# Modulation rows of a one-core backbone layer: the sum over k on GpSimd, one matmul by ones on TensorE

## The reference, cut to what matters

```python
mod_lat = (jax.nn.silu(c) @ w_mod[l] + b_mod[l])[:, None, :]
sh1, sc1, gt1, sh2, sc2, gt2 = jnp.split(mod_lat, 6, axis=-1)
...
yx, _, _ = _token_mixer(hx, st_fwd, st_bwd, True, True, **mp)
x = x + gt1 * _rmsnorm(yx, ng[1])
...
hx = _modulate(_rmsnorm(x, ng[2]), sh2, sc2)
x = x + gt2 * _rmsnorm(_peer(hx, ...), ng[3])
```

## Time and profile before

| | |
|---|---|
| median of 3 runs | 2881.05 us (2877.75 to 2894.06) |
| span of the profiled execution, the only time that is known of it | 3458.3 us |
| granted TensorE clock in it | 0.555 |
| TensorE busy | 3369.1 us (97%) |
| VectorE busy | 1668.8 us (48%) |
| GpSimd busy | 1188.9 us (34%) |
| ScalarE busy | 614.5 us (18%) |
| stage 4 in it | about 530 to 1480 us |

### The profile page before, as it was taken

How to read it: one execution, slowest core, us unless ns; L and a number is a source line. 1 busy time by engine, 2 the same in 40 slices (tenths; PEclk the granted TensorE clock), 3 DMA queues, 4 the chain that set the end, 5 groups by cost and what they waited for, 6 DMA issues and landing times.

```text
span 3458.3 us, 29585 instructions
## 1 busy us (share of the span) xinstructions
PE 3369.1 (97%) x8354; PEld 1703.9 (49%) x8354; DVE 1668.8 (48%) x3954; ACT 614.5 (18%) x1385; POOL 1188.9 (34%) x1143
## 2 busy tenths in 40 slices
PE   8999999999999999989899999999999999999998
PEld 3333327999999999935533333222222222222222
DVE  1167503455545455452533443466555555555661
ACT  2043200011011110121111111212222221222121
POOL 3000000000000000000444434767676877677772
PEclk6555555555555555555555555555555555555555
DMA  4122212122111111041777766889997999889994
GB/s 153 33 83 98 86 36 73 37 54 69 37 50 37 49 38 37 13 152 36 253 264 260 276 223 227 316 306 361 352 338 284 346 360 350 307 334 364 342 334 158
DMA packets 266271, 650.77 MB, mean 188 GB/s; under 512 B 21280, under 2 KB 120192, under 8 KB 265856
## 3 DMA queue, kind: packets, MB, share of 16 engines
q0 software_dynamic: 150336, 552.67, 44.0%
q1 hardware_dynamic: 115776, 96.28, 9.3%
HBM read 631.04 MB, written 17.83 MB: 188 GB/s over the span
## 4 chain that ended last, share of the span: by engine, by line
PE 96%; DMA 2%; ACT 1%; issue 1%; DVE 1%; SPq 0%; ACTq 0%; DVEq 0%; PEldq 0%
PE bank L1269 46%; PE bank L1749 10%; PE bank L780 5%; PE bank L765 5%; PE bank L778 4%; PE bank L1281 4%; PE bank L963 3%; PE bank L718 3%; PE bank L1751 2%; PE bank L1722 1%; PE bank L739 1%; PE bank L688 1%; PE bank L1014 1%; PE bank L786 1%; PE bank L750 1%; PE bank L745 1%
## 5 line engine op out<-in xcount | busy, mean ns | idle before, releaser
L1269 PE MATMUL bank<-arena 128*128 128x512 f32 x2048 | 1577.5, 967 | 25.6 <-DVE arena L1231 19.5
L1269 PEld LDWEIGHTS bank<-arena 128*128 128x128 f32 x2048 | 464.0, 227 | 1130.4 <-issue 1114.1
L1250 DVE CUSTOM_DVE_ANT_0 arena<-arena 128x1024 f32<-128x1024 f32 x512 | 608.5, 1225 | 537.2 <-DMA arena<-in_peer_u_dram,arena 537.2
L1062 POOL DMA_INDIRECT arena<-in_peer_v_dram,arena x512 | 577.0, 1127 | 364.7 <-PE bank L1269 222.6
L1062 POOL DMA_INDIRECT arena<-in_peer_u_dram,arena x512 | 565.3, 1104 | 302.6 <-issue 135.9
L1095 ACT ACTIVATE arena<-arena 128x128 f32<-128x128 f32 x512 | 201.8, 401 | 1172.1 <-PE bank L1269 1164.2
L1749 PE MATMUL bank<-arena 128*128 128x512 f32 x432 | 349.6, 968 | 6.2 <-PEq L381 3.5
L825 POOL MEMSET arena<- 128x4096 f32 x1 | 3.5, 3517 | 954.8 <-DVE arena L613 954.8
L780 PE MATMUL bank<-arena 128*128 128x128 f32 x960 | 207.3, 392 | 0.0
L765 PE MATMUL bank<-arena 128*128 128x128 f32 x960 | 197.1, 384 | 0.1
L780 PEld LDWEIGHTS bank<-arena 128*128 128x128 f32 x960 | 194.6, 302 | 0.0
(11 more groups left out here) (279 smaller groups left out, 2668.6 us busy)
## 6 DMA issues: line engine op xcount, KB each, us to landing
arena<-in_w_mod_dram SPq DMA_DIRECT2D x24, 1024.0 KB, 6.2
arena<-in_peer_wq_dram SPq DMA_DIRECT2D x32, 512.0 KB, 6.4
arena<-in_w_in_dram SPq DMA_DIRECT2D x27, 512.0 KB, 4.1
arena<-kr_scratch SPq DMA_DIRECT2D x96, 128.0 KB, 3.5
arena<-in_peer_u_dram,arena POOLq DMA_INDIRECT x512, 6.1
arena<-in_peer_v_dram,arena POOLq DMA_INDIRECT x512, 6.1
bk_scratch<-arena POOLq DMA_DIRECT2D x8, 768.0 KB, 3.6
kr_scratch<-arena POOLq DMA_DIRECT2D x8, 768.0 KB, 5.0
```

Of the source, the lines that this page charges most:

```text
L1062: pool.indirect_dma_start(ring[:, j % RING, :], None, table, bass.IndirectOffsetOnAxis(ap=idx[:, hi % 4, j:j + 1].bitcast(U32), axis=0)).t ...
L1250: nc.vector.tensor_tensor_reduce(u_ring[:, j % RING, :], u_ring[:, j % RING, :], h2cur, 1.0, 0.0, ALU.mult, ALU.add, acts[:, h % 2, j:j + ...
L1269: m = nc.tensor.matmul(PO[h][:, :], diag[:, j % 4], v_ring[:, j % RING, 512 * h:512 * h + 512], start=hp == 0 and j == 0, stop=hp == HEADS ...
```

## The change

GpSimd now multiplies the loaded block by silu(c), in place, and adds up its eight values of k in three halving steps, the last of them into `row_sum`, which has two buffers. TensorE does one matmul, with a 128x128 tile of ones, which sums over the partitions and spreads the result. `row_steps` counts GpSimd's steps, four for a row: TensorE waits for the fourth instead of the weights' landing, and SP's next load of `wmr` waits for GpSimd's fourth step instead of TensorE's matmul. GpSimd waits for the matmul of two rows earlier before it writes `row_sum`. The `silb` tile and its copy are gone; `ones` takes one memset more. No instruction changes its place against others on an engine.

```diff
     wmr = cut(KT, 256)
-    silb = cut(KT, P)
+    row_sum = cut(2, 256)
+    ones = cut(P)
+    cut = Cut(MOD + 2048 + D, ARENA - 2048)
     rows = cut(4, D)
...
-                    sp.wait_ge(modulation_rows, 4 * p + j)
+                    sp.wait_ge(row_steps, 16 * p + 4 * j)
                     apart(sp)
                 sp.dma_start(wmr, wmod_v[:, :, bass.ds(p * D + (2 * D + 256 * j), 256)]).then_inc(wmod_row_weights, 16)
...
-        nc.gpsimd.tensor_copy(silb, silu_col[:, :, 0:1].broadcast_to([P, KT, P])).then_inc(silu_spread, 1)
+        nc.gpsimd.memset(ones, 1.0).then_inc(n_zeroed, 1)
+
+        def weighted_row(p, j, first):
+            n = 4 * p + j
+
+            pool.wait_ge(wmod_row_weights, 16 * n + 16)
+            nc.gpsimd.tensor_tensor(wmr, wmr, silu_col[:, :, 0:1].broadcast_to([P, KT, 256]), ALU.mult).then_inc(row_steps, 1)
+            pool.wait_ge(row_steps, 4 * n + 1)
+            nc.gpsimd.tensor_tensor(wmr[:, 0:4], wmr[:, 0:4], wmr[:, 4:8], ALU.add).then_inc(row_steps, 1)
+            pool.wait_ge(row_steps, 4 * n + 2)
+            nc.gpsimd.tensor_tensor(wmr[:, 0:2], wmr[:, 0:2], wmr[:, 2:4], ALU.add).then_inc(row_steps, 1)
+            pool.wait_ge(row_steps, 4 * n + 3)
+            if not (first and j < 2):
+                pool.wait_ge(modulation_rows, n - 1)
+            nc.gpsimd.tensor_tensor(row_sum[:, j % 2], wmr[:, 0], wmr[:, 1], ALU.add).then_inc(row_steps, 1)
+
+        def do(p, b, chain, first):
+            for j in MOD_BLOCKS[b]:
+                weighted_row(p, j, first)
+        steps4(pool, do, lambda: None)
...
             if first and j == 0:
-                pe.wait_ge(silu_spread, 1)
+                pe.wait_ge(n_zeroed, 7)
...
-            pe.wait_ge(wmod_row_weights, 64 * p + 16 * j + 16)
-            for k in range(KT):
-                m = nc.tensor.matmul(C1[j % 2][:, P:P + 256], silb[:, k, :], wmr[:, k, :], start=k == 0, stop=k == KT - 1)
-            m.then_inc(modulation_rows, 1)
+            pe.wait_ge(row_steps, 16 * p + 4 * j + 4)
+            nc.tensor.matmul(C1[j % 2][:, P:P + 256], ones, row_sum[:, j % 2], start=True, stop=True).then_inc(modulation_rows, 1)
```

More of the change, by code:

```diff
@@ L322, in _layer @@
     wmod_row_weights = sem("wmod_row_weights")
-    silu_spread = sem("silu_spread")
+    row_steps = sem("row_weighting_steps")
     modulation_rows = sem("modulation_rows")
```

## The result

| | before | changed |
|---|---|---|
| median of 5 runs each | 2885.37 us | 2906.59 us |
| ratio, 95% interval | | 1.0076 [1.0048, 1.0104] |
| span of the profiled execution | 3458.3 us | 2905.0 us |
| mean granted clock in it | 0.555 | 0.900 |

The change makes the kernel slower by 21 us, 0.76%, outside the forecast range. The two profiled executions can't be laid side by side: that of the kernel before ran with a mean granted clock of 0.555 and took 3458.3 us. Every later execution of it had 0.907 to 0.965. The clock of its five timed runs wasn't recorded, but they were as short (2877.75 to 2894.06 us) as the later ones on the first chip, which had 0.91 (2866.42 to 2901.19 us). The first experiment therefore profiles the kernel before again.

What follows compares the result with a forecast made beforehand. TensorE, busy 97%, was taken to bound the kernel, with only work to win. Heads 15 plus third-block slots 18 minus collisions 2 gave 31 us less, 2881 - 31 = 2850 us (-1.1%), range 2818 to 2878.

Steps and rivals of the forecast that it cites:

- 15 + 18 - 2: Stage 4: 15 us saved in block heads, 18 in the third blocks' slots, 2 lost to collisions, 31 us less.
- What bounds the kernel, and the clock of the runs: Whole kernel: TensorE busy 97%, no idle time to win; runs need 0.83 of the profiled time, estimated clock 0.67.
- The remark that the expert stage could shorten by at most a sixth: Expert stage: already moves 304 GB/s against 364 in its best slice, so other stages may have run faster than 0.67.
- The slot in the head: Block heads, 12 of 16 rows: VectorE's chain of 12.4 us becomes the limit; 1.4 us saved each, 11 counted, 15 us.
- VectorE is already the limit: Rival, in the heads: from a clock of 0.74 the twelve head slots give nothing; 2865 to 2873 us, 25 in 100.
- The slot in the third block: Third blocks, 4 rows: VectorE has little to do, so the whole 4.5 us a row is saved, 18 us.
- GpSimd's price: GpSimd in stage 4: two reads an element, 7.8 us a row, hidden except at the first row, counted as nothing.
- In the way: VectorE beside GpSimd in stage 4: only the last, short sums meet an L587; 2 us charged, ends nothing and 30.
- the narrow collision: GpSimd holds up only L587, at most 1.9 us a row; rival where every one is held: 2878 us, 5 in 100.
- its own sign of it: In the changed profile: L587 exceeding 0.35 us often would show the forecast wrong by narrow collision.
- the bound of 30: Upper end of the collision charge in stage 4: 16 rows at 1.9 us each.
- The wide collision: Rival: GpSimd's reads hold up every VectorE instruction, PSUM operand or not; 2891 to 2930 us, 10 in 100.

Runs made afterwards that it cites:

- The first experiment: The kernel before, unchanged, profiled again at the clock of the runs: 2890.79 us in one run, stage 4 621.7 us.
- where it stood alone: Against the kernel before: no GpSimd sums, constant rows, one matmul in the third blocks' four slots, eight in the heads: 0.9934, stage 4 612.3 us.
- the example above: Timeline of one block's head in the changed kernel: one matmul at 419.59, 2.02 us idle, clock at 0.5 from 422.2 to 429.0; whole kernel 1.0076.
- beside the eight matmuls: The kernel before with its eight matmuls a row, plus GpSimd's four operations a row into a tile nobody reads: 2918.02 us, stage 4 640.9.
- filled heads and thin slots: The changed kernel with its GpSimd sums, the matmul by ones repeated eight times in each head, once in the third blocks' second slot: 1.0054, stage 4 646.3 us.

## Why the prediction was wrong

The forecast was 31 us less; measured were 21 us more. The sum "15 + 18 - 2" failed in all three of its terms, and a fourth was missing. The heads gave nothing instead of 15 us, because the clock of the runs was wrong; the third blocks' slots gave 9.4 instead of 18; the collisions cost 15.3 us of stage 4 instead of 2; and a lower clock behind the thinned heads, which the sum had at nothing without a word on it, cost 13.3. The first mistake alone would have left a gain; it is the last two that turned the sign.

**What bounds the kernel, and the clock of the runs: the first step that failed.** The prediction took the whole's ratio of 0.83 as one factor for TensorE's work and arrived at a clock of 0.67. The clock of later executions as short as the runs is 0.91, and 0.98 in stage 4. The ratio was a mixture: from the first profile to the second one of the same kernel, the part up to the end of stage 4 went from 1489.5 to 979.7 us (0.66), the part behind it from 1968.8 to 1909.5 (0.97). The remark that the expert stage could shorten by at most a sixth was the right one, and was given too little weight: it shortened by 3%.

**The slot in the head.** The mechanism was right, VectorE's chain takes over at about 12.4 us. Since the clock was higher, it had taken over already: at full clock TensorE's path is 16.66 x 0.555 = 9.2 us by its own scaling, and 10.15 measured. The 15 us of the sum were nothing; this was the rival "VectorE is already the limit", given 25 in 100.

**The slot in the third block.** 3.0 us at full clock for seven matmuls, 12 in four slots; measured 9.4 where it stood alone. In the changed kernel a low clock lay over part of it.

**What no step had:** that less work in the head lowers the clock behind it, 13.3 us. The prediction read the clock as a given of the execution, and so never asked what the thinned heads would do to it. The Trainium skill (TensorE: Matmul & The Clock Gate, Part 1) has TensorE's clock follow its activity, down to half. The traces agree in the levels (1.0 and 0.5) and in what goes before the fall, an idle or thin stretch of the engine (2.02 us in the example above); the 0.555 of the first profile is in none of its levels.

**GpSimd's price** was right in its total (7.8 us a row, measured 8.0), in part by luck: the four instructions were put at 4.2, 2.1, 1.0 and 0.5 us and took 3.61, 2.36, 1.27 and 0.73, so that a first one that was too dear made up for three that were too cheap. Its place was right too: TensorE waits for it once, at the first row, 4.4 us.

**In the way.** The mechanism was the narrow collision that the prediction priced, and its own sign of it came: 27 of the 88 L587 take more than 0.40 us, where none did before. The charge of 2 us was the wrong end. The holds came to 31.6 us in L587 and cost 15.3 us of stage 4, and to 43.1 us and 19.2 beside the eight matmuls, within the bound of 30. So about half of the holding doesn't reach the time of the stage. Two things made the charge too small. The prediction placed the sums among the rounds of the slow profile, 11.6 us each, and concluded that only the last short sums meet an L587; a round is 6.7 us at the clock of the runs, shorter than a row's 8.0, and 14 pairs in 16 rows are met. And it took the cost of one collision as that of the longest instruction, where the two L587 of a pair can be held by two instructions of GpSimd in turn, 3.47 us instead of 0.61 at the worst place of the changed kernel. The wide collision didn't occur.

**The sum, redone:** -9.4 (slots) + 13.3 (clock) + 15.3 (holds) = +19.2 us, measured 19.3 in stage 4, 21 in the whole. What this tests is that the first two add up (625.6 against 625.7); the third is the difference that is left. The holds have no single price: they cost 15.3 us of stage 4 beside thin heads, 19.2 in the kernel before, and 34.0 beside filled heads and thin slots (646.3 - 612.3), 14.0 of it in the first block. The rivals were priced one at a time; two of them came true together, and the term of the clock was missing.

## What to carry to other kernels

Before costing work taken off an engine, make sure that the profile was taken at the clock of the timed runs, and if the two times differ, work out the ratio stage by stage: work that is on the path at half clock can be free at full clock. Work of TensorE that hides behind another engine may be what keeps its clock up, so it is better used (here by giving it more columns) than removed. GpSimd is a free helper beside a busy VectorE only as long as it doesn't read SBUF while VectorE has instructions with two SBUF inputs on its path; if it must, short instructions bound each hold. And effects that were measured one at a time needn't add up when they come together: the filled heads brought the clock back and the stage was longer.

## What the runs showed of the hardware

In the example above the clock fell at the end of 2 us without a matmul, behind a head in which TensorE had been busy for 6 us until then; with the eight matmuls in the same place, and gaps of 1.27 and 0.84 us behind them, it stayed at 1.0. Whether the gap or the thin stretch as a whole brings it down isn't separated.

A VectorE instruction with two inputs in SBUF was held by a GpSimd instruction that reads SBUF, up to 3.4 us for 0.35, and never by a memset of the same length. A VectorE instruction with an input in PSUM was held by neither.

The kernel before ran with a granted clock of 0.555 for a whole execution, and with 0.907 to 0.965 in every later one. The 0.555 isn't a mean of 0.5 and 1.0: windows of 4 us at 100, 300 and 900 us of that execution all have 0.56, and between them it fell to 0.50 for a few us at a time. What sets this wasn't tried.

Two chips differed by 9% on the same program (2883.46 and 2629.09 us for the kernel before), and not in stage 4: that of the changed kernel took 641.0 and 640.4 us, what comes behind it 1908.2 and 1639.5. Why wasn't tried.
